# Scaling and adding the second value row of each pair on GpSimd in tiles 0 to 5 of a hybrid encoder layer

## What is computed

```
q = (xb @ w_q).reshape(blk, PEER_HEADS, 2, PEER_DHALF)
s = jnp.einsum('thpc,hpkc->thpk', q, sub_keys)
...
top, pos = lax.top_k(cand, PEER_TOPK)
idx = jnp.take_along_axis(cidx, pos, axis=-1)
g = jax.nn.softmax(top, axis=-1)
u = jnp.take(u_tab, idx, axis=0)
a = jax.nn.gelu(jnp.einsum('thkd,td->thk', u, xb), approximate=False)
w = (g * a).astype(xb.dtype)
return jnp.einsum('thk,thkd->td', w, jnp.take(v_tab, idx, axis=0))
```

## Time and profile before

| | us |
|---|---|
| median of 3 runs (lowest, highest) | 4839.9 (4837.3, 4844.48) |
| the profiled execution, its own time | 4842.08 |
| its span | 4840.1 |
| span until the first gather (L1772) | 415.67 |
| `finish` of tiles 0, 2, 5, 7 (L1721) begins at | 1184.70, 2415.88, 3951.93, 4611.94 |

### The profile page before, as it was taken

The page is one execution under the profiler, slowest core; times in us unless marked ns, Lnnn a source line. Parts: engine busy times, 40 slices in busy tenths (PEclk is TensorE's granted clock), DMA queues, the critical chain, the costliest instruction groups (busy, mean ns, idle before and its releaser), DMA issues.

```text
span 4840.1 us, 36330 instructions
## 1 busy us (share of the span) xinstructions
PE 3931.8 (81%) x11755; PEld 2003.8 (41%) x11755; DVE 2343.3 (48%) x5664; ACT 1694.9 (35%) x4064; POOL 1171.0 (24%) x1122
## 2 busy tenths in 40 slices
PE   5676877997998869999799899578989977777755
PEld 4463455743444545544344455334543322322211
DVE  1212352326336643434544577453444466666665
ACT  1211253323216643432332366353433233333322
POOL 0001111113221211212332232132222244444422
PEclk8788987999998889999999999789999999999988
DMA  7377756779876786778988798797888899999977
GB/s 247 133 257 268 260 192 228 272 292 381 302 283 236 267 297 253 275 271 314 383 337 336 292 353 307 242 351 282 321 308 315 322 408 421 419 412 418 420 278 280
DMA packets 296691, 1480.38 MB, mean 306 GB/s; under 512 B 42597, under 2 KB 112229, under 8 KB 145909
## 3 DMA queue, kind: packets, MB, share of 16 engines
q0 software_dynamic: 156672, 1140.92, 60.6%
q1 hardware_dynamic: 139828, 337.14, 19.5%
HBM read 1411.39 MB, written 66.56 MB: 305 GB/s over the span
## 4 chain that ended last, share of the span: by engine, by line
PE 54%; DMA 17%; DVE 10%; ACT 7%; issue 6%; POOL 2%; SPq 1%; POOLq 0%; DVEq 0%; ACTq 0%
PE c_p_y L1228 22%; DMA c_ring<-in_uv,l_idx 10%; DVE c_ring L1711 5%; PE c_PB L962 4%; PE c_PC L962 4%; PE c_PA L1170 3%; PE c_PA L1215 2%; PE c_PB L1215 2%; PE c_PC L1170 2%; PE c_PB L1170 2%; POOL c_ring L1772 2%; ACT l_diag L1400 2%; DMA c_area<-oT_sp 1%; PE c_PA L1198 1%; ACT l_wgt L1395 1%
## 5 line engine op out<-in xcount | busy, mean ns | idle before, releaser
L1228 PE MATMUL c_p_y<-c_ring,l_diag 128*128 128x512 f32 (+1 forms) x4352 | 2116.6, 633 | 422.3 <-ACT l_diag L1400 421.8
L1772 POOL DMA_INDIRECT c_ring<-in_uv,l_idx x1088 | 1164.4, 1070 | 3512.7 <-PE c_p_y L1228 2917.2
L1711 DVE CUSTOM_DVE_ANT_0 c_ring<-c_ring,l_h_cur 128x1024 f32<-128x1024 f32 x1088 | 1296.1, 1222 | 398.5 <-DMA c_ring<-in_uv,l_idx 341.8
L1228 PEld LDWEIGHTS c_p_y<-c_ring,l_diag 128*128 128x128 f32 (+1 forms) x4352 | 832.8, 198 | 1572.8 <-issue 936.7
L1392 ACT ACTIVATE l_gel<-l_dots 128x2 f32<-128x2 f32 x544 | 110.6, 203 | 1552.6 <-DVE l_dots L1711 1551.1
L1400 ACT ACTIVATE l_diag<-c_ident,l_wgt 128x128 f32<-128x128 f32 x1024 | 355.0, 394 | 16.7
L1392 ACT ACT_TABLE_LOAD x208 | 266.9, 1283 | 47.1 <-DVE l_dots L1711 43.7
L1395 ACT ACTIVATE l_wgt<-l_gel,l_gw 128x1 f32<-128x1 f32 x1088 | 261.0, 287 | 17.9
L962 PE MATMUL c_PC<-c_area 128*128 128x451 f32 (+1 forms) x576 | 226.2, 545 | 5.4 <-DMA c_area<-in_w_in 5.4
L962 PE MATMUL c_PB<-c_area 128*128 128x451 f32 (+1 forms) x576 | 227.2, 548 | 3.4 <-DMA c_area<-in_w_in 2.2
L1170 PE MATMUL c_PA<-c_area 128*128 128x128 f32 (+3 forms) x512 | 131.5, 413 | 118.9 <-DMA c_area<-oT_sp 114.7
(11 more groups left out here) (283 smaller groups left out, 3669.7 us busy)
## 6 DMA issues: line engine op xcount, KB each, us to landing
c_area<-in_w_gb SPq DMA_DIRECT2D x32, 2304.0 KB, 9.4
c_area<-in_w_in SPq DMA_DIRECT2D x32, 1804.0 KB, 8.5
c_area<-rw_sp SPq DMA_DIRECT2D x16, 2048.0 KB, 9.3
c_ring<-in_uv,l_idx POOLq DMA_INDIRECT x1088, 8.8
c_area<-in_w_out SPq DMA_DIRECT2D x8, 2048.0 KB, 8.8
proj<-c_area SPq DMA_DIRECT2D x64, 225.5 KB, 4.9
c_area<-proj SPq DMA_DIRECT2D x8, 1288.0 KB, 5.7
c_ring<-in_w_qT SPq DMA_DIRECT2D x16, 512.0 KB, 7.3
```

The source lines that it names most:

```text
L1228: ins = mm_(p_y[:T, e * 512:(e + 1) * 512], diag[:, j, :T], ring[:, j, D + e * 512:D + (e + 1) * 512], start=r == 0 and q == 0 and k == 0, ...
L1711: ins = nc.vector.tensor_tensor_reduce(out=ring[:, j, 0:D], in0=ring[:, j, 0:D], in1=h_cur[:, :], scale=1.0, scalar=0.0, op0=ALU.mult, op1 ...
L1772: nc.gpsimd.indirect_dma_start(out=ring[:, j, :], out_offset=None, in_=t_in["uv"][:, :], in_offset=bass.IndirectOffsetOnAxis(ap=idx[:, hea ...
```

## The change

In groups 0 to 2 (tiles 0 to 5, 384 pairs; `apart(n)` is true for them) GpSimd scales the v half of each pair's second row in place by `wgt` and adds it to `ysb`. TensorE multiplies and ScalarE makes `diag` for the first row only. GpSimd does this for pair n - 1 just ahead of the gathers of pair n + 3, and these now wait for its own addition (`s_vapart`) too. `ysb` has two buffers, and x1 is loaded into one before the tile begins. To make room in SBUF, `mkT` and `mv` move into the shared area and are loaded again for each group (a DMA of 512 KB each, for which TensorE waits at the memory scores, `s_mkv`), and the scratch tiles of the top-k search share memory.

```diff
+def apart(n):
+    return ALL_PAIRS[n][0] < GROUPS[-1][0]
...
@@ prepare, SyncE
+            sp.wait_ge(s_mkT, 1)
+            sp.dma_start(mkT_sp[:, :], mkT[:, :]).then_inc(s_put, 16)
...
@@ layer
-    sc_rep = sb("sc_rep", [128, 256])
-    cand = sb("cand", [128, TOPK * TOPK])
-    cand_rep = sb("cand_rep", [128, TOPK * TOPK])
+    onehot = sb("onehot", [128, 2, TOPK, TOPK])
+    cand, cand_rep = (onehot[:, k, :, :].rearrange("p a b -> p (a b)") for k in range(2))
+    sc_rep = cand_rep
...
-    ysb = sb("ysb", [128, D])
+    ysb = [sb(f"ysb{k}", [128, D]) for k in range(2)]
...
@@ mix, SyncE
             if k == 0 and t == first_of(g):
                 projected(g)
                 load_P(t)
+                sp.dma_start(mkT[:, :, :].rearrange("p h k -> p (h k)"), mkT_sp[:, :]).then_inc(s_mkv, 16)
+                sp.dma_start(mv[:, :, :], outs["mem_v"].rearrange("(a p) n -> p a n", p=128)).then_inc(s_mkv, 16)
...
@@ pair, SyncE
-                if r == 4:
-                    if i:
-                        sp.wait_ge(s_out, 16 * i)
-                    sp.wait_ge(s_spill[i % 2], 32 * (i // 2 + 1))
-                    sp.dma_start(ysb[:width_of(i), :], x1[rows(i), :]).then_inc(s_xres, 16)
+                if r == HEADS - 1 and i + 1 < NT:
+                    load_x1(i + 1)
...
@@ pair, TensorE
             pe.wait_ge(s_diag, n + 1)
-            for k in range(PAIR):
+            for k in range(1 if apart(n) else PAIR):
...
@@ weigh, ScalarE
             act.wait_ge(s_ae, n_e + 1)
+            if n >= 8 and apart(n - 8):
+                act.wait_ge(s_vapart, apart_before(n - 7))
...
-            for k in range(PAIR):
+            for k in range(1 if apart(n) else PAIR):
                 ins = nc.scalar.mul(diag[:, (n * PAIR + k) % RING, :T], unit[:, :T], wgt[:, c0 + k:c0 + k + 1])
...
@@ finish, VectorE
+            if apart(pair_index(i, r, q)):
+                dve.wait_ge(s_vapart, apart_before(pair_index(i, r, q) + 1))
...
@@ gather, GpSimd
                 pool.wait_ge(s_vdone, n - RING // PAIR + 1)
+                if apart(n - RING // PAIR):
+                    pool.wait_ge(s_vapart, apart_before(n - RING // PAIR + 1))
...
+        def values(n):
+            if n < 0 or not apart(n):
+                return
+            i, r, q = ALL_PAIRS[n]
+            T, j, col = width_of(i), (n * PAIR + 1) % RING, q * PAIR + 1
+            if r == 0 and q == 0:
+                pool.wait_ge(s_xres, 16 * (i + 1))
+            if n:
+                pool.wait_ge(s_vapart, apart_before(n))
+            pool.wait_ge(s_diag, n + 1)
+            y = ysb[i % 2]
+            v = ring[:T, j, D:2 * D]
+            nc.gpsimd.tensor_scalar(out=v, in0=v, scalar1=wgt[:T, col:col + 1], scalar2=None,
+                                    op0=ALU.mult).then_inc(s_vscaled, 1)
+            pool.wait_ge(s_vscaled, apart_before(n) + 1)
+            nc.gpsimd.tensor_tensor(out=y[:T, :], in0=v, in1=y[:T, :], op=ALU.add).then_inc(s_vapart, 1)
...
         def pair(i, r, q):
             n = pair_index(i, r, q) + LEAD
+            values(n - LEAD - 1)
             if n < len(ALL_PAIRS):
                 gather(n)
```

More of the change, by code:

```diff
@@ L77, in pair_index, with apart_before @@
     return (i * HEADS + r) * 8 + q if i < TILES else TILES * HEADS * 8 + r * 4 + q
+def apart(n):
+    return ALL_PAIRS[n][0] < GROUPS[-1][0]
+def apart_before(n):
+    return sum(apart(k) for k in range(n))
 ALL_PAIRS = [(i, r, q) for i in range(NT) for r in range(HEADS) for q in range(pairs_of(i))]
@@ L225, in h3, with prepare @@
     return ap.rearrange("p (h d) -> p h d", h=h)
-def prepare(nc, c, t_in, outs, rw_sp, ctx):
+def prepare(nc, c, t_in, outs, rw_sp, mkT_sp, ctx):
     m = Scope(nc, ctx, "r")
@@ L391, in mem @@
                     act.wait_ge(s_km, 1)
-                    nc.scalar.copy(c.mkT[:, :, :].rearrange("p h k -> p (h k)"), c.PA[:, :]).then_inc(s_mkT, 1)
+                    nc.scalar.copy(mkT[:, :], c.PA[:, :]).then_inc(s_mkT, 1)
             def route(k):
@@ L512, in layer @@
     gaT = flat(18768, 128, GRANK)
+    mkT = cube(18896, MH, NMEM)
+    mv = cube(19920, MT, BW)
     g_hT = cube(A0, DT, 384)
@@ L603, in layer @@
     s_slot = [sem(f"slot{k}") for k in range(RING)]
-    s_dot, s_diag, s_vdone = (sem(n) for n in ("dot", "diag", "vdone"))
+    s_dot, s_diag, s_vdone, s_vapart, s_vscaled = (sem(n) for n in ("dot", "diag", "vdone", "vapart", "vscaled"))
     s_dl, s_de, s_al, s_ae = (sem(n) for n in ("dl", "de", "al", "ae"))
@@ L892, in load_h, with load_x1 @@
                 sp.dma_start(h_cur[T:2 * T, :], h_sp[rows(i), :]).then_inc(s_hcur, 16)
+        def load_x1(i):
+            if i >= 2:
+                sp.wait_ge(s_out, 16 * (i - 1))
+            sp.wait_ge(s_spill[i % 2], 32 * (i // 2 + 1))
+            sp.dma_start(ysb[i % 2][:width_of(i), :], x1[rows(i), :]).then_inc(s_xres, 16)
         def start():
@@ L1010, in mix @@
                     pe.wait_ge(s_mkT2, 1)
+                else:
+                    pe.wait_ge(s_mkv, 32 * (next(g for g in range(len(GROUPS)) if t in GROUPS[g]) + 1))
                 for h in range(MH):
@@ L1720, in finish @@
             dve.wait_ge(s_xres, 16 * (i + 1))
-            tt(out=ysb[:T, :], in0=p_y[:T, :], in1=ysb[:T, :], op=ALU.add).then_inc(s_yev, 1)
+            if apart(pair_index(i, r, q)):
+                dve.wait_ge(s_vapart, apart_before(pair_index(i, r, q) + 1))
+            y = ysb[i % 2]
+            tt(out=y[:T, :], in0=p_y[:T, :], in1=y[:T, :], op=ALU.add).then_inc(s_yev, 1)
         def pick(n, piece):
@@ L1814, in program @@
             ("x1", (TOKENS, D)), ("h_sp", (TOKENS, D)), ("sc_sp", (TOKENS, 16 * NK)), ("rw_sp", (4, 128, DT * 512)),
-            ("kT_sp", (2, FH, AD, SEQ)))]
+            ("kT_sp", (2, FH, AD, SEQ)), ("mkT_sp", (128, MH * NMEM)))]
         constants(nc, c)
         with ExitStack() as inner:
-            prepare(nc, c, t, out, dram[6], inner)
+            prepare(nc, c, t, out, dram[6], dram[8], inner)
         layer(nc, c, t, out, dram, ctx)
```

20 lines of the change are left out of this document (10 added, 10 removed).

## The result

The changed kernel takes 5126.23 us (median of 3 runs, 5116.37 to 5133.82) against 4839.9 us: a ratio of 1.059, 95% interval 1.056 to 1.062. It is 5.9% slower, where 4.5% faster was forecast, and lies far above the range (4460 to 4850).

A forecast was written before the change was run, and what follows sets the result against it. TensorE was taken to set the pace in tiles 0 to 5, the transfers in the tails. -63 - 126 - 94 - 60 + 86 + 32 + 5 = -220 from 4840 gave 4620 us, range 4460 to 4850.

The forecast's parts named there:

- The terms on TensorE's side: Savings from TensorE's shorter work: dense stretches of groups 0, 1, 2 -63, -126, -94 us, mixer steps -60.
- GpSimd's cap of 7.0 us: GpSimd's time per pair, 6.4 us undisturbed and 7.0 with VectorE beside it, below which group 2's pace could not go.
- the price of the scaling: GpSimd's scaling of 128x1024, put at 1.12 us by a line through small copy and select rows.
- My upper bound of 6.2 us: Upper bound for GpSimd's scaling and addition together, with the addition at 4.95 ns a column; 3.55 us was taken.
- My sign: In the profile after, GpSimd's two instructions taking much over 3.5 us together would mean contention for the SBUF port.
- Tails: The last 16 pairs of each group, without front work: from the DMA pace of 5.2 to 7.0 us, +86 us.
- Group 2: Its dense stretch of 103 pairs, at a pace of 8.3 us, would save 94 us.
- Groups 0 and 1: Their dense stretches, 36 and 76 pairs at paces of 14.2 and 10.4 us, would save 63 and 126 us.
- Rival 3: GpSimd becomes the pace of everything behind tile 2, its period 8.8 us: slower, about 5040 us, chance 0.13.
- The port: GpSimd's SBUF reads beside VectorE's dots: chance overlap of 1.2 us a pair, half borne by each side.
- Rival 2: Port shared by whole instructions, GpSimd's period 7.6 us and dots late: about 4836 us, no change, chance 0.20.
- The clock: TensorE's granted clock falls by a tenth more in the mixer stretches as it idles more: +32 us.

The follow-up runs named there:

- run 3: The changed kernel with GpSimd's scaling and addition cut to one column, all waits kept: 4518.36 us, ratio 0.935 to the kernel before.
- run 1: The changed kernel with every value row kept on TensorE, leaving only the buffer changes and reloads: 4840.95 us, ratio 1.001 to the kernel before.
- run 2: The kernel before with GpSimd memsets, copy, scalings and addition of 128x1024 run alone in the constants: scaling by pointer 2.84 us, addition 2.34, copy 1.04.
- run 5: The changed kernel with both rows kept on TensorE in the last two heads of groups 0 to 2: 4950.92 us, ratio 1.024 to the kernel before.
- run 6: The changed kernel with GpSimd's two instructions only in groups 0 and 1, outside their last two heads: 4743.69 us, ratio 0.980 to the kernel before.
- run 4: The changed kernel with five memsets for GpSimd's scaling and an addition of one column: 5005.4 us, ratio 1.036 to the kernel before.
- runs 7 and 8: The changed kernel with the scaling on ScalarE, 4701.71 us; the same with two memsets and a one-column addition for GpSimd's addition, 4611.88 us.
- run 11: The changed kernel with each of GpSimd's two instructions cut into four of 256 columns: 5675.8 us, in one run only.

## Why the prediction was wrong

**What bounds the kernel** was right where it said so. TensorE was the pace in tiles 0 to 5: halving the pairs' matmuls with GpSimd free saves 320 us (run 3). The terms on TensorE's side, 63 + 126 + 94 + 60 less 32 for the clock and 5 for the reloads, came to 306. That they had GpSimd's cap of 7.0 us in them for group 2 and the run had not makes the agreement partly luck: without a cap I expected 400 (run 3's expectation), and it is 320. By group, dense and mixer pairs together and before the clock, the forecast had 69, 144 and 130, and run 3 saved 68, 113 and 134. The reloads at +5 and the other edits at 0 hold (run 1: 1 us).

**The step that failed is the price of the scaling**, "235 + 960 x 0.92 = 1.12 us". It costs 2.84 (run 2). The slope came from a copy and a select, and the copy indeed costs 1.04 at this size, but a multiplication is not a copy on this engine. The trace of before held no arithmetic instruction of one input on GpSimd. The only arithmetic row was the addition of 64 columns, 82 ns above the copy of the same size, and a bound for the scaling should have reached to it. My upper bound of 6.2 us for the two stretched only the addition (to 5.07), where the line was good to 4%, and left the scaling at 1.12. The 5.18 of both alone lie inside it by luck. So GpSimd's period was put at 6.4, or 7.0 with the port, and is 8.5 to 9.0. Of the 2.1 us from 6.4 to the 8.5 of the timeline above, the two instructions are 1.65 (1.74 for the scaling, 0.09 less for the addition). Most of the rest is a second, smaller term: I put the three waits between GpSimd's own instructions at 0.3 us together, and the one ahead of the gather is 0.77 by itself. My sign "over 3.5 together by much means the port" would have misled too: run 2 shows 5.18 with nothing beside them.

From that the other terms follow. **Tails**: forecast 48 x 1.8 = +86, measured +175 (run 5), by a pace of 9.03 and not 7.0. **Group 2**: forecast -94 in its dense part and about -36 in its mixer part, measured +259 in all, some 60 of it the tail. **Groups 0 and 1**: the forecast gave their fronts -63 and -126 and the mixer steps' part; run 6 shows what both instructions gain there, 96 us together with the mixers (24 of the forecast), under half of it. Run 3, with GpSimd free, saves 181 us in these two groups, so about half of their relief is lost to GpSimd's instructions. The three items miss the forecast by 89, 326 and 117 us; the 37 us for clock and reloads are already in the measured stretches, which leaves 495 of the 506 us between 4620 and 5126.

**Rival 3 is what happened**, by the mechanism that it named: with a period of 8.8 us it gave 5040, and it put the turning point at 7.8. (By its own terms the upper bound gives 2.5 + 6.2 + 0.3 = 9.0; 8.8 is the case of all dots waited out.) Its +173 for the tails and its 100 us saved in groups 0 and 1 agree with the 175 of run 5 and the 96 of run 6. Run 6 bears the mechanism out from the other side, since the sign turns with the pace. It too came out low, by 86 us. It counted group 2 at 8.8 - 8.3 = 0.5 us a pair, as if the pace were even; the front pairs there take (1795 - 16 x 9.03) / 176 = 9.4 us. My reading, which no run tests, is that a period of 8.5 to 9.0 binds wherever the pace of the moment was below it, and that the time saved elsewhere doesn't come back through a ring of 4 pairs. A mean pace of 8.3 hides both.

**The port** was priced at 0.6 us a pair on GpSimd. It went mostly the other way round: GpSimd waits little (the median addition is at 2.35 us, its price alone 2.34; the mean is 2.52 and the longest 4.85, and the scaling's mean 2.94 against 2.84, so 0.3 us a pair), and VectorE waits more, its dots at 1703 ns in tiles 3 to 5. The sum of its effect is 121 us beside the long GpSimd work (runs 3 and 4 and the change) and 90 beside the short (runs 7 and 8). Rival 2 had this mechanism (where the prediction speaks of the third rival, the second is meant). The rule of the Trainium skill ("SBUF — State Buffer", "Who interferes with whom"), that a VectorE instruction of two SBUF inputs contends with a GpSimd instruction that reads SBUF and not with one that only writes it, agrees for the addition: the dot at 4156.29 waits to its end, cutting the instructions in four cuts the longest wait (run 11), and memsets, which read nothing, leave the dots at 1223 ns (run 4). Its clause on VectorE's two-port modes, which a cast or a scaling by a scalar can enter and which contend with GpSimd, agrees with the cast that took 1.63 us beside the scaling and with those that waited behind run 4's memsets. What the traces do not bear out is a lock for the whole instruction where GpSimd scales: the dots that begin 1 us or more into a scaling take 1.23 us, and the small scaling at 4161.48 ended 1.7 us before GpSimd's did. Why the scaling holds the dots only at its start was not tried. The luck is not equal either, as I had assumed: VectorE loses more.

**The clock** fell further than the tenth that I took in the mixers alone: 0.79 in group 2 and 0.62 in its tail, where TensorE idled two thirds of the time. The mean of the pairs' matmuls went from 633 to 724 ns. I take this for a consequence and not a cause, since TensorE waits there anyway: they are 4.4% of the chain in tiles 3 to 5, and the matmuls of the input projection (L982, before L962) went there only from 542 to 553 ns. No run separates it. How much of the missing 80 us in run 3 (granted clock 0.872 against 0.918) is the clock was not tried either.

## What to carry to other kernels

Price an instruction that is to move to another engine by a row of the same operation on that engine, or measure it by itself first; a row of a copy says nothing of a multiplication, and a bound that stretches only the safer of two instructions holds by luck. When an engine also issues the transfers that pace the kernel, add its new work to its issue time and compare the sum with the pace of every stretch, not with the mean: here the same two instructions gain 2% where the pace was 10 us or more and lose where it was 8.3 or 5.2. Choose the places by that (the tails left alone, the scaling on an engine that does it in 1.13 us) and the idea is worth 3.3%.

## What the runs showed of the hardware that I had not expected

- On GpSimd a `tensor_scalar` multiplication of 128x1024 float32 takes 2.78 us by a constant and 2.84 by a pointer, longer than a `tensor_tensor` addition (2.34), and 2.7 times a copy (1.04).
- Four additions of 256 columns take 3.7 us for one's 2.5, four scalings 4.0 for 2.9, in the mean beside VectorE's work (by the medians 2.9 for 2.35, and 3.7 for 2.86).
- Between an addition on GpSimd and the indirect DMA behind it stand 0.77 us of idle time, where two DMAs are 0.30 apart.
- A dot of VectorE that began while GpSimd added lost up to 2.2 us (3394 ns against 1222): it ended 1.08 us after the addition. One that began 1 us or more into a scaling took 1.23 us in the mean. GpSimd lost 0.3 us a pair.
- Memsets on GpSimd left the dots at 1223 ns, but VectorE's small scalings and casts of one input took up to 1.03 us beside them (medians of 0.17 to 0.18 in run 3).
